# Low-rank projection inside the first value projection of the GLA stage, with that stage's event order written anew

## The reference

```
proj = h @ W_in                      # 512 q, 512 k, 512 v, 512 z for attention; 256 q, 256 k, 512 v, 512 z for GLA;
                                     # 16 low-rank columns; 2 x 1024 gate columns
o_sb  = stick_breaking(q, k, v)      # 8 heads x 64, strictly causal
alpha_logit = lr @ w_alpha_up + b_alpha_up           # lr: the 16 low-rank columns
log_alpha   = log_sigmoid(alpha_logit) / 16
# GLA, 4 heads (dk 64, dv 128), chunks of 64 rows
cum = cumsum(log_alpha, within the chunk)
q_dec, k_inv, k_to_end = q*exp(cum)*scale, k*exp(-cum), k*exp(cum_last - cum)
o_intra = tril(q_dec @ k_inv.T) @ v ; kv = k_to_end.T @ v
S_next = exp(cum_last) * S + kv      # a recurrence over 16 chunks
o_gla = rmsnorm(o_intra + q_dec @ S)
m = sigmoid(g_A) * ((o_sb * silu(z_sb)) @ w_o_sb) + sigmoid(g_B) * ((o_gla * silu(z_gla)) @ w_o_gla)
y = RMSNorm_final(x + m @ W_out)
```

## Time and profile before

| | us |
|---|---|
| median of 3 runs | 800.51 (800.15 to 800.85) |
| the profiled execution | 799.51 |
| its span | 797.8 |
| TensorE busy in the span | 787.5 (99%) |
| VectorE busy | 581.0 (73%) |
| ScalarE busy | 410.4 (51%) |
| GpSimd busy | 30.7 (4%) |
| mean granted TensorE clock | 0.999 |

### The profile page before, as it was taken

The page is one execution under the profiler, slowest core; times in us unless marked ns, Lnnn a source line. Parts: engine busy times, 40 slices in busy tenths (PEclk is TensorE's granted clock), DMA queues, the critical chain, the costliest instruction groups (busy, mean ns, idle before and its releaser), DMA issues.

```text
span 797.8 us, 11836 instructions
## 1 busy us (share of the span) xinstructions
PE 787.5 (99%) x4424; PEld 668.1 (84%) x4424; DVE 581.0 (73%) x828; ACT 410.4 (51%) x710; POOL 30.7 (4%) x30
## 2 busy tenths in 40 slices
PE   8999999999999999999999999999999999999997
PEld 7778888888888888889889888888888888888886
DVE  6528997989798798954646655655557777779986
ACT  7526675766667566663263153344333333465443
POOL 1540000000000000020000000000000000000000
PEclk9999999999999999999999999999999999999999
DMA  9862012212300220021110001233433333395222
GB/s 322 283 224 53 27 28 53 53 27 53 77 26 26 53 53 27 28 80 53 54 53 1 28 28 53 92 130 135 158 119 106 106 105 106 106 366 214 106 106 106
DMA packets 72483, 76.31 MB, mean 96 GB/s; under 512 B 3804, under 2 KB 57207, under 8 KB 71928
## 3 DMA queue, kind: packets, MB, share of 16 engines
q1 hardware_dynamic: 72242, 75.45, 29.7%
q10 hardware_dynamic: 198, 0.28, 0.1%
HBM read 55.79 MB, written 15.73 MB: 90 GB/s over the span
## 4 chain that ended last, share of the span: by engine, by line
PE 92%; ACT 4%; DVE 2%; issue 1%; DMA 0%; DVEq 0%; ACTq 0%
PE pj L704 27%; PE tr L1007 5%; PE ob L955 5%; PE sc L955 5%; PE pj L847 4%; PE ob L795 4%; PE ob L1007 4%; PE pj L1007 4%; PE tr L805 4%; PE sc L1007 3%; PE pj L720 3%; PE pj L828 3%; PE sc L771 2%; PE sc L770 2%; PE tr L1063 1%; PE ob L1033 1%
## 5 line engine op out<-in xcount | busy, mean ns | idle before, releaser
L704 PE MATMUL pj<-h_lo,w_hi 128*128 128x512 f32 x336 | 133.1, 396 | 0.0
L704 PE MATMUL pj<-h_hi,w_lo 128*128 128x512 f32 x336 | 132.2, 393 | 0.0
L704 PE MATMUL pj<-h_hi,w_hi 128*128 128x512 f32 x336 | 132.1, 393 | 0.0
L1711 DVE TENSOR_TENSOR_SCAN surv<-surv,diag 128x128 f32<-128x128 f32 (+3 forms) x64 | 86.3, 1349 | 7.4 <-ACT surv L1197 7.2
L704 PEld LDWEIGHTS pj<-h_hi,w_hi 128*128 128x128 f32 x336 | 63.1, 188 | 12.8 <-issue 0.2
L704 PEld LDWEIGHTS pj<-h_hi,w_lo 128*128 128x128 f32 x336 | 63.2, 188 | 12.6 <-issue 0.5
L704 PEld LDWEIGHTS pj<-h_lo,w_hi 128*128 128x128 f32 x336 | 63.1, 188 | 12.5 <-issue 0.3
L1241 ACT ACTIVATE wt_hi<-tr 128x512 fp32r<-128x512 f32 (+2 forms) x96 | 43.6, 490 | 36.6 <-PE tr L805 35.1
L1635 DVE TENSOR_TENSOR w_lo<-w_raw,w_hi 128x1024 fp32r<-128x1024 f32 x33 | 40.3, 1222 | 26.5 <-ACT w_hi L1129 26.2
L1744 DVE TENSOR_TENSOR wt_lo<-tr,wt_hi 128x512 fp32r<-128x512 f32 (+2 forms) x96 | 50.2, 550 | 7.1 <-ACT wt_hi L1241 6.4
L1715 DVE TENSOR_TENSOR beta<-beta,surv 128x128 f32<-128x128 f32 (+3 forms) x64 | 48.6, 759 | 6.5
(11 more groups left out here) (426 smaller groups left out, 1907.3 us busy)
## 6 DMA issues: line engine op xcount, KB each, us to landing
w_raw<-in_w_in SPq DMA_DIRECT2D x30, 512.0 KB, 3.8
y_scratch<-y_ring SPq DMA_DIRECT2D x28, 256.0 KB, 2.0
graw<-in_w_in SPq DMA_DIRECT2D x14, 512.0 KB, 5.0
y_back<-y_scratch SPq DMA_DIRECT2D x14, 512.0 KB, 5.2
x_t<-in_x SPq DMA_DIRECT2D x8, 512.0 KB, 6.2
wrow<-in_w_out SPq DMA_DIRECT2D x4, 1024.0 KB, 7.8
w_scratch<-wsum SPq DMA_DIRECT2D x4, 1024.0 KB, 4.6
wout_raw<-in_w_out SPq DMA_DIRECT2D x8, 512.0 KB, 7.4
```

Source lines behind the costliest of these rows:

```text
L704: mm = pe.matmul(pj[bank][:, :], (w_lo if p == 2 else w_hi)[:, slot, k, :], (h_lo if p == 1 else h_hi)[:, k, HALF * h:HALF * h + HALF], st ...
L1711: dve.tensor_tensor_scan(s[:, ::-1], s[:, ::-1], d[:, ::-1], 0.0, ALU.mult, ALU.add)\
```

## The change

The low-rank projection leaves the opening. Its 16 weight columns are loaded late in the last pair (`lr_raw`), split into 16 high and 16 low columns that lie behind the 256 value columns in `vn_hi`, and v0's products with `vn_hi` have 288 moving columns. v0 is evacuated after each of its 8 row tiles: ScalarE copies the 256 value columns, VectorE the 32 others to `lr_nat`. Two turns (`lrt`) bring those into `lr_p`. So `alpha` of hp 0 can't run in z0 any more: it stands in z1, and every later event has a new position. The k of the second GLA pair goes to `stage_q` instead of `stage_k`. In the opening, half 1 goes k, q, v, and the waits for the `wsum` stores go to steps 1 and 2 of the first pair.

```diff
-BANKS = {"z0": 38, "v0": 40, "z1": 44, "k1": 46, "v1": 48, "z2": 52, "z3": 54}
+BANKS = {"z0": 38, "v0": 40, "z1": 48, "k1": 50, "v1": 52, "z2": 56, "z3": 58}
+V_UNITS = {"v0": 8, "v1": 4}
...
-        mix("z0", [(("pre", 20), 0), (("alpha", 0), 2), (("pre", 21), 8), (("log1", 0), 26)])
-        + mix("v0", [(("log2", 0), 2), (("decay", 0), 50), (("end", 0), 52), (("pre", 22), 60), (("pre", 23), 100),
-                     (("kt", 0, 0), 150), (("kt", 0, 1), 156)])
-        + mix("z1", [(("sc", 0), 3), (("kv", 0), 5), (("st", 0, 0, 8), 6), (("pre", 24), 12), (("st", 0, 8, 15), 25),
-                     (("pre", 25), 34)])
-        + mix("k1", [(("o", 0), 6), (("norm", 0), 16), (("pre", 26), 30)])
-        + mix("v1", [(("alpha", 1), 4), (("pre", 27), 12), (("log1", 1), 20), (("log2", 1), 50), (("decay", 1), 98),
-                     (("end", 1), 100), (("kt", 1, 0), 176), (("kt", 1, 1), 182)])
-        + mix("z2", [(("out", 0, 0), 1), (("out", 0, 1), 3), (("out", 0, 2), 8), (("out", 0, 3), 13), (("sc", 1), 17),
-                     (("kv", 1), 19), (("st", 1, 0, 8), 20), (("st", 1, 8, 15), 26)])
-        + mix("z3", [(("pre", 28), 4), (("o", 1), 10), (("norm", 1), 25)])
+        mix("z0", [(("pre", 20), 0), (("pre", 21), 8), (("pre_lr",), 14)])
+        + mix("v0", [(("pre", 22), 60), (("pre", 23), 100)])
+        + mix("z1", [(("lrt",), 4), (("pre", 24), 5), (("alpha", 0), 8), (("log1", 0), 25)])
+        + mix("k1", [(("log2", 0), 2), (("pre", 25), 25), (("decay", 0), 25), (("end", 0), 26)])
+        + mix("v1", [(("kt", 0, 0), 4), (("kt", 0, 1), 12), (("sc", 0), 18), (("kv", 0), 20), (("st", 0, 0, 8), 21),
+                     (("pre", 26), 30), (("st", 0, 8, 15), 31), (("o", 0), 64), (("norm", 0), 97), (("pre", 27), 98),
+                     (("alpha", 1), 124), (("log1", 1), 145)])
+        + mix("z2", [(("out", 0, 0), 1), (("out", 0, 1), 4), (("log2", 1), 6), (("decay", 1), 25), (("end", 1), 26),
+                     (("out", 0, 2), 36), (("out", 0, 3), 40)])
+        + mix("z3", [(("kt", 1, 0), 1), (("kt", 1, 1), 6), (("sc", 1), 11), (("pre", 28), 12), (("kv", 1), 14),
+                     (("st", 1, 0, 8), 15), (("st", 1, 8, 15), 18), (("o", 1), 32)])
+        + [("norm", 1)]
...
@@ SyncE
-            sp.dma_start(lr_raw[:, :, :], w_in_v[:, :, COL_LR:COL_LR + RANK]).then_inc(lr_loaded, 16)
...
+            twin(0, 1)
             store_wsum(2)
             store_wsum(3)
-            twin(0, 2)
...
+                if n == 21:
+                    sp.wait_ge(proj_free, BANKS["z0"] - 6)
+                    sp.dma_start(lr_raw[:, :, :], w_in_v[:, :, COL_LR:COL_LR + RANK]).then_inc(lr_loaded, 16)
@@ TensorE, opening
-            for k in range(KT):
-                turn_x([KT + k] if k < 3 else [])
-                low_rank(0, k)
+            turn_x(range(KT, KT + 3))
             first_tile(2, 2, 0, [(11, 0), (12, 2), (13, 4), (14, 6)])
             turn_x([15])
-            for n in range(2):
-                first_tile(n, 3 + n, 1, [])
+            first_tile(1, 3, 1, [])
+            first_tile(0, 4, 1, [])
             first_tile(2, 5, 1, [])
-            for k in range(KT):
-                low_rank(1, k)
-            pe.wait_ge(lr_out, 2)
@@ TensorE, value_product
+                width = 2 * DV + (2 * RANK if name == "v0" and p != 1 else 0)
+                moving = vn_lo[k // 4][:, k % 4, :] if p == 1 else vn_hi[:, k, 0:width]
@@ TensorE, GLA events
+                elif kind == "lrt":
+                    n = R3 + TURN[ev]
+                    pe.wait_ge(proj_free, BANKS["v0"] + V_UNITS["v0"])
+                    pe.wait_ge(tr_free, n - 1)
+                    for g in range(2):
+                        mm = pe.transpose(tr[n % 2][:, P * g:P * g + P],
+                                          lr_nat[:, 4 * g:4 * g + 4, :].rearrange("p j r -> p (j r)"), ident[:, :])
+                    mm.then_inc(tr_ready, 1)
@@ ScalarE, opening
-            lr_quarters(1)
-            for k in range(4):
+            for k in range(2):
                 act.wait_ge(wsum_stored[k], 16)
+            act.wait_ge(wsum_done, 16)
@@ ScalarE, GLA events
+                    act.wait_ge(dve_step, 3)
+                    stage(stage_q, c, u, u)
```

More of the change, by code:

```diff
@@ L144, in turn_numbers @@
     for ev in gla_events():
-        if ev[0] in ("kt", "out"):
+        if ev[0] in ("lrt", "kt", "out"):
             numbers[ev] = at
@@ L298, in stickbreak_gla_hybrid, with v_rows @@
         first7 = [tr[0], tr[1], ob[0], ob[1], sc[:, 0:HALF], sc[:, HALF:2 * HALF], pj[1]]
+        def v_rows(hp, b):
+            if hp == 0:
+                return v_nat[:, b, :]
+            return v_alt[:, b, :] if b < ST // 2 else v_nat[:, b - ST // 2, :]
         def x_bank(r):
@@ L723, in first_tile @@
                 mm.then_inc(proj_ready, 1)
[L725 to L734, removed]
             for t in range(4):
@@ L839, in value_product @@
             def value_product(name, m):
-                u, t, k, p = m // 48, m // MM_HALF, m % MM_HALF // 3, m % 3
-                c = BANKS[name] + u
+                t, k, p = m // MM_HALF, m % MM_HALF // 3, m % 3
+                per = ST // V_UNITS[name]
+                c = BANKS[name] + t // per
                 if m == 0:
                     pe.wait_ge(lo_done, V_TILES[name][1] + 1)
-                if m % 48 == 0:
+                    pe.wait_ge(lr_split, 2)
+                if m % (per * MM_HALF) == 0:
                     pe.wait_ge(proj_free, c - 1)
[L847 to L851, removed]
+                width = 2 * DV + (2 * RANK if name == "v0" and p != 1 else 0)
+                c0 = 256 * (t % per)
+                moving = vn_lo[k // 4][:, k % 4, :] if p == 1 else vn_hi[:, k, 0:width]
+                mm = pe.matmul(pj[c % 2][:, c0:c0 + width], (h_lo if p == 2 else h_hi)[:, k, P * t:P * t + P], moving,
+                               start=(k == 0 and p == 0), stop=(k == KT - 1 and p == 2), skip_group_check=True)
+                if m % (per * MM_HALF) == per * MM_HALF - 1:
                     mm.then_inc(proj_ready, 1)
@@ L870, in _ @@
                         pe.wait_ge(o_free, 2 + 8 * PAIRS)
+                        pe.wait_ge(tr_free, R3 + TURN["lrt",] + 1)
                     else:
@@ L900, in _ @@
                     pe.wait_ge(tr_free, R3 + TURN["kt", hp, 1] + 1)
[L901 removed]
+                    name = "v1" if hp else "v0"
+                    pe.wait_ge(proj_free, BANKS[name] + V_UNITS[name])
                     for c in range(NCH - 1):
@@ L906, in _ @@
                             mm = pe.matmul(kvs[HD * e:HD * e + HD, :], k_end[row:row + CH, b, HD * e:HD * e + HD],
-                                           v_nat[row:row + CH, b, DV * e:DV * e + DV], start=True, stop=True,
+                                           v_rows(hp, b)[row:row + CH, DV * e:DV * e + DV], start=True, stop=True,
                                            skip_group_check=True)
@@ L1162, in _ @@
             high_part(1, 1, 1, None, None)
[L1163 to L1166, removed]
+            row_norms(range(4, 7))
             act.wait_ge(raw2_loaded, 16)
@@ L1171, in _ @@
             stage(stage_k, 1, 0, 1)
-            h_high(range(KT, KT + 3))
-            lr_quarters(0)
-            h_high(range(KT + 3, R0))
+            h_high(range(KT, R0))
             stage(v_t, 2, 0, 0)
-            stage(stage_q, 3, 1, 1)
-            stage(stage_k, 4, 1, 0)
+            stage(stage_k, 3, 1, 1)
+            act.wait_ge(proj_free, 4)
+            stack(0, 1)
+            high_part(3, 1, 2, proj_ready, 4)
+            stage(stage_q, 4, 1, 0)
             act.wait_ge(proj_free, 5)
-            for part in range(2):
-                stack(0, part)
-            high_part(3, 1, 2, proj_ready, 5)
+            stack(0, 0)
             stage(v_t, 5, 1, 1)
-            lr_quarters(1)
-            for k in range(4):
+            for k in range(2):
                 act.wait_ge(wsum_stored[k], 16)
+            act.wait_ge(wsum_done, 16)
             def pair(i, last):
@@ L1201, in pair @@
                                        ACT.Sigmoid, scale=HD ** -0.5).then_inc(sig_done, 1)
+                    if step in (1, 2):
+                        act.wait_ge(wsum_stored[step + 1], 16)
                     for n, r in enumerate(ROUNDS):
@@ L1676, in _ @@
             low_part(1, 1)
[L1677 to L1681, removed]
+            norm_rows(range(4, 7))
             dve.wait_ge(hi_done, 3)
@@ L1687, in _ @@
             stage(stage_k, 1, 0, 1)
-            h_low(range(KT, KT + 3))
-            lr_quarters(0)
-            h_low(range(KT + 3, R0))
+            h_low(range(KT, R0))
             stage(v_t, 2, 0, 0)
-            stage(stage_q, 3, 1, 1)
-            stage(stage_k, 4, 1, 0)
+            stage(stage_k, 3, 1, 1)
             dve.wait_ge(wsum_stored[1], 16)
-            for part in range(2):
-                stack(0, part, part)
+            stack(0, 1, 0)
             low_part(3, 1)
+            stage(stage_q, 4, 1, 0)
```

(24 more changed lines are left out.)

73 lines of the change are left out of this document (35 added, 38 removed).

## The result

The changed kernel takes 807.23 us, the median of 6 runs (805.52 to 808.35), against 799.91 us for the kernel before (6 runs, 798.79 to 800.85). The ratio is 1.009, 95% interval 1.0075 to 1.0105: slower by 7.3 us. The forecast was 803.0, in the right direction, but its change of +2.5 us is a third of the measured one; 807.2 lies inside the range and outside case A's own. One of run 5's ten executions took 2790.98 us; it counts as slow and is left out of that run's ratio, and its median without it is 798.09.

What follows compares the result with a forecast made beforehand. TensorE's own work, busy 99% of the span, was taken to bound the kernel. Opening -7.8, z0 and v0 -0.5, z1 to z3 +10.9 sum to +2.6 us on 800.51, so 803.0 us; range 798.5 to 808.

Steps and rivals of the forecast that it cites:

- case A: Main forecast for the whole kernel: all terms summed, 803.0 us, own range 801 to 805.5; chance 0.52.
- The opening: Start to first pair: removing the low-rank matmuls gains 7.8 us; the k and q swap costs no matmul.
- Rival F: At the first pair: it waits for twin or wsum, up to 3.7 us back, 806.7 us; chance 0.07.
- v0: Value products: 128 matmuls widened from 256 to 288 columns cost 1.7 us, by interpolation between 256 and 512.
- rival E: In v0: 288 columns cost as much as 512, +12 us, so 815 us; chance 0.03.
- The chain: z1 to z3: GLA events come too early for their inputs, +10.9 us, of which 9.5 are stalls.
- o(0): First GLA head pair's output: waits 3.4 us for the last state, starting 38.5 us after z1 starts.
- alpha(1): Second GLA head pair's alpha: waits 1.7 us for the first pair's norm, at 53.5 us after z1 starts.
- o(1): Second GLA head pair's output: waits 4.0 us for the last state, starting 90.6 us after z1 starts.
- rival D: Behind the two long stalls: TensorE's clock falls, 2 x 2.7 = 5.4 us more, 808.4 us; chance 0.10.
- B: Rival for z1 to z3: the GLA chain keeps up with TensorE, so 793.6 us; chance 0.10.
- C: Rival for z1 to z3: half the stalls, -2.2 us, so 798.3 to 800 us; chance 0.18.

Runs made afterwards that it cites:

- run 5: Kernel before without low-rank products, q before k and wsum waits ahead of the first pair, plus 45 identity turns in TensorE's wait for k's twin: 798.26 us.
- run 3: Kernel before with the changed opening alone: no low-rank products, k before q, wsum waits in steps 1 and 2: 792.59 us.
- run 1: Changed kernel with identity turns (27, 12 and 38) filling TensorE's three long waits, before o(0), alpha(1) and o(1): 802.08 us.
- run 2: Changed kernel with positions alone moved in v1 and z3, so matmuls lie where TensorE waited: 793.02 us.
- run 6: Changed kernel with identity turns in the two long waits before o(0) and o(1), the short one before alpha(1) left idle: 801.69 us.
- run 7: Changed kernel with z3's positions alone moved: split of tile 28 behind the state updates, o(1) from 32 to 46: 800.44 us.
- run 4: Kernel before without low-rank products, but with q before k and all wsum waits ahead of the first pair as before: 800.73 us.

## Why the prediction was right, and what it sized wrong

The direction and the waits came out as forecast. What failed is a term of the sum: the low clock behind the waits was put at nothing and cost 5.1 us. The gain of the opening was put 0.5 to 0.7 us too high.

**The opening** was put at -7.8. Run 3 gives -7.1. The profile shows -6.4, partly because one of x's row tiles landed late (ScalarE waits 0.7 us for it):

```profile
ACT junk L1112 <- DMA x_t<-in_x: 0.7, 1, 0.7
```

In run 1, with the same opening, there is no such wait and the first pair starts at 51.11, 7.3 us earlier than at first. So the lateness is not in every execution of that opening. But five of its six profiles have it (0.6 to 1.3 us; runs 2, 3, 6 and 7 beside the changed kernel), and none of the three with q before k, though the lists of runs 3 and 4 are the same up to there. So the rival in run 3's expectation, that the change brings it, is not refuted; the tile is the third one that ScalarE takes, not the second. Even without it 7.3 us are gained and not 7.8. One reason shows in run 1's profile: the 0.3 us wait for x is still 0.34, where 0.2 of it was to go.

Rival F did not come: TensorE has no wait at the first pair, so k's twin was home in time. That this hung on the order of k and q, and not by little, run 4 shows; the prediction gave the swap no price ("costs no matmul"), though undoing it, with the `wsum` waits, costs 8.1 us. The other half of F came close. The prediction had GpSimd's last addition end at 48.96, 1.6 us before the first pair. In the changed kernel it ends at 51.72 + 1.29 = 53.01, behind the pair's first matmul: the last eight additions start 1.0 us later than before, and two of them stretch by 2.1 and 1.0 us while VectorE makes its splits of k, of a weight tile and of q:

```profile
43.55 3.37 POOL L653 TENSOR_TENSOR wsum<-wrow,wsum 128x512 f32<-128x512 f32 x1
...
49.38 2.26 POOL L651 TENSOR_TENSOR wsum<-wrow,wsum 128x512 f32<-128x512 f32 x1
...
51.72 1.29 POOL L653 TENSOR_TENSOR wsum<-wrow,wsum 128x512 f32<-128x512 f32 x1
```

ScalarE waits 0.6 us for it and TensorE not at all. That the margin was gone and cost nothing is luck.

**v0** was put at 1.7 us for the wider products. Its three products in turn, in TensorE's timeline:

```profile
347.27 0.30 PE L839 MATMUL pj<-vn_hi,h_lo 128*128 128x288 f32 x1
347.40 0.30 PE L839 MATMUL pj<-vn_hi,h_hi 128*128 128x288 f32 x1
347.54 0.28 PE L839 MATMUL pj<-vn_lo,h_hi 128*128 128x256 f32 x1
347.65 0.30 PE L839 MATMUL pj<-vn_hi,h_lo 128*128 128x288 f32 x1
```

Steps of 0.13 and 0.14 after the wide ones and 0.11 to 0.12 after the narrow; all 192 take 24.53 us against 23.0 at 0.120, so +1.5. The interpolation between 256 and 512 columns held (a step of about 0.133); rival E is out. z1 starts 0.95 us earlier than at first beyond the opening, where 0.5 was forecast.

**The chain**, step by step, counted from z1's start at 371.17:

| event | forecast | measured | step forecast | step measured |
|---|---|---|---|---|
| sc(0) | 26.5 | 26.3 | 26.5 | 26.3 |
| o(0) | 38.5 | 38.2 | 12.0 | 11.9 |
| alpha(1) | 53.5 | 55.8 | 15.0 | 17.6 |
| sc(1) | 78.6 | 82.5 | 25.1 | 26.6 |
| o(1) | 90.6 | 94.7 | 12.0 | 12.3 |
| end of z3 | 100.3 | 106.1 | 9.7 | 11.3 |

The places and lengths of the three long waits came out as forecast: 3.0, 1.6 and 4.0 us for 3.4, 1.7 and 4.0. The three steps that are too long, by 2.6, 1.5 and 1.6, are those that hold TensorE work at the low clock: o(0), the first v1 products after alpha(1), and o(1).

What sets the steps to o(0) stands in VectorE's timeline, as in the earlier trace rows: four masked copies, a weight split, and the state updates in two lots.

```profile
398.64 3.01 DVE L1856 COPY_PREDICATED sT<-mask,tr 64x512 f32<-64x512 int32 x4 [1.25 <-PE tr L890]
...
405.06 1.22 DVE L1633 TENSOR_TENSOR w_lo<-w_raw,w_hi 128x1024 fp32r<-128x1024 f32 x1
406.20 3.05 DVE L1870 SCALAR_TENSOR_TENSOR state<-state,stats,ob 128x128 f32<-128x128 f32 x7
```

They end at 409.25, and o starts at 409.39.

**The clock** is the step that was weighed wrongly. The prediction had it as rival D with a chance of 0.10 and left it out of the sum; run 1 shows that it costs 5.1 us, and without them the kernel would be slower by 2.4 us and not by 7.3. That D's 5.4 us come so near is partly luck. D counted two falls of 2.7 us. The profile has 2.6 in o(0), 1.6 in o(1), and 1.5 behind alpha(1), where D had none. The 2.7 itself was half of the 24 turns' 5.38 us; by the prediction's own rows these turns would take 24 x 0.09 = 2.2 us at the full clock, so the start cost 3.2. The rule taken from the Trainium skill (page "TensorE: Matmul & The Clock Gate", section "Why this matters for your kernels") is borne out here: behind the waits of 3.0 and 4.0 us the clock is 0.50 to 0.58 in the windows above, and with the waits filled or moved away it is 1.00. That no row of before showed such a wait was no evidence that it would be harmless. A and D together would have been 808.4, 1.2 over the measurement, and A alone is 4.2 under it.

**Rivals B and C** fell in the changed kernel: its waits are A's. B's number is nearly that of run 2: the price was right, what was missing were positions that let the chain keep up.

## What to carry to other kernels

When work that served as cover is taken off the path, redo the positions of every wait behind it: lay the chain's step (here sc to o, 11.9 us of VectorE) beside the bound engine's work in between (8.6 us), one pair at a time. Look for a second price behind each wait of TensorE, in the clock of the work right behind it: here waits of 8.6 us in all brought 5.1 us more. And an order that costs nothing by count (k before q) can be what makes a removal pay at all.

## What the runs showed of the hardware beyond that

- Turns of the identity kept the granted clock at 1.00 through waits of 3.0, 4.0 and 4.6 us (runs 1 and 5); 27 of them took 3.11 us, 38 took 4.31 and 45 took 5.07.
- In run 4 VectorE's split of q took 2.28 us beside a GpSimd addition that took 1.29; in run 5 the same split took 1.22 and the addition beside it 2.35. In the changed kernel the additions at 43.55 and 49.38 took 3.37 and 2.26 us, where they take 1.29 in the earlier trace rows, and the split of q 1.72. So when the two overlap either of them can be the one that stretches.
- In five of six profiles of the changed opening ScalarE waited 0.6 to 1.3 us for one of x's row tiles. The first pair started at 51.11 us in the one without that wait and at 51.59 to 52.32 us in the others.
